# Latent attention on one core: queries, keys and values from the ranks as three products of rounded halves

## The reference, cut to what matters

```python
MLA_HEADS, MLA_Q_RANK, MLA_KV_RANK = 16, 384, 256
MLA_NOPE, MLA_ROPE, MLA_V = 64, 32, 64
def project(h, rotate):
    cq, ckv, kr, gate = split_last(h @ w_in, (MLA_Q_RANK, MLA_KV_RANK, MLA_ROPE, MLA_WIDTH))
    q = (rms_norm(cq, q_norm_g) @ w_uq).reshape(b, n, MLA_HEADS, MLA_NOPE + MLA_ROPE)
    kv = (rms_norm(ckv, kv_norm_g) @ w_ukv).reshape(b, n, MLA_HEADS, MLA_NOPE + MLA_V)
    ...
oc = attention_blocks(qc, kc, vc)                                   # context attends to itself
ox = attention_blocks(qx, concat([kc, kx]), concat([vc, vx]))       # input attends to both
return out(oc, gc), out(ox, gx)                                     # (o * silu(gate)) @ w_out
```

## Time and profile before

| | |
|---|---|
| time, median of 3 runs | 1775.43 us (1773.72 to 1776.09) |
| the profiled execution | 1776.33 us, of which the span is 1774.3 |
| TensorE (PE) busy | 1686.1 us, 95% of the span |
| VectorE (DVE) busy | 1323.5 us, 75% |
| ScalarE (ACT) busy | 777.0 us, 44% |
| DMA | 331.92 MB, mean 187 GB/s |

### The profile page before, as it was taken

The page is one execution under the profiler, slowest core; times in us unless marked ns, Lnnn a source line. Parts: engine busy times, 40 slices in busy tenths (PEclk is TensorE's granted clock), DMA queues, the critical chain, the costliest instruction groups (busy, mean ns, idle before and its releaser), DMA issues. The chain is left out here.

```text
span 1774.3 us, 30736 instructions
## 1 busy us (share of the span) xinstructions
PE 1686.1 (95%) x13112; PEld 1512.1 (85%) x13112; DVE 1323.5 (75%) x1965; ACT 777.0 (44%) x997; POOL 6.3 (0%) x14
## 2 busy tenths in 40 slices
PE   2999989999999999999899999999999999999998
PEld 2999978888899989999798779999886555759898
DVE  7777788855877778998878557999767768567844
ACT  2433365323633354343753327343652345355354
POOL 0000000000000000000000000000000000000000
PEclk9999999999999999999999999999999999999999
DMA  9868536351577746885364435776153200223102
GB/s 390 340 270 305 207 108 246 133 202 63 203 305 285 282 180 271 321 316 198 119 227 155 179 128 207 273 279 229 48 213 143 95 34 15 107 95 143 48 24 96
DMA packets 48807, 331.92 MB, mean 187 GB/s; under 512 B 5256, under 2 KB 8480, under 8 KB 9376
## 3 DMA queue, kind: packets, MB, share of 16 engines
q1 hardware_dynamic: 47808, 326.79, 48.2%
q0 software_dynamic: 864, 3.17, 0.7%
HBM read 328.87 MB, written 1.07 MB: 186 GB/s over the span
## 5 line engine op out<-in xcount | busy, mean ns | idle before, releaser
L347 PE MATMUL ps<-xhi,low 128*128 128x256 f32 x2048 | 499.5, 283 | 4.2 <-ACT xhi L1459 4.2
L347 PEld LDWEIGHTS ps<-xhi,low 128*128 128x128 f32 x2048 | 360.5, 190 | 6.4 <-ACT xhi L1459 5.6
L347 PE MATMUL ps<-xhi,whi_wk 128*128 128x256 f32 x1072 | 298.5, 288 | 40.5 <-ACT xhi L1459 38.7
L347 PE MATMUL ps<-xlo,whi_wk 128*128 128x256 f32 x1072 | 291.5, 281 | 0.0
L1459 ACT ACTIVATE wk<-ps 128x256 f32<-128x256 f32 (+5 forms) x219 | 108.1, 503 | 386.8 <-PE ps L347 320.8
L1459 ACT ACTIVATE whi_wk<-ring 128x2048 fp32r<-128x2048 f32 x100 | 191.6, 1918 | 195.3 <-DMA ring<-in_stream_dram 145.2
L347 PEld LDWEIGHTS ps<-xhi,whi_wk 128*128 128x128 f32 x1072 | 203.5, 195 | 43.2 <-issue 41.8
L2068 DVE TENSOR_TENSOR low<-ring,whi_wk 128x2048 fp32r<-128x2048 f32 (+1 forms) x101 | 228.4, 2264 | 6.6 <-ACT whi_wk L1459 6.6
L347 PE MATMUL ps<-wk 64*64 64x64 f32 (+10 forms) x2712 | 210.3, 262 | 5.8 <-ACT wk L1459 4.3
L347 PEld LDWEIGHTS ps<-wk 64*64 64x64 f32 (+4 forms) x2712 | 162.3, 146 | 55.0 <-issue 29.5
L347 PEld LDWEIGHTS ps<-xlo,whi_wk 128*128 128x128 f32 x1072 | 197.9, 189 | 0.0
(11 more groups left out here) (141 smaller groups left out, 2861.7 us busy)
## 6 DMA issues: line engine op xcount, KB each, us to landing
ring<-in_stream_dram SPq DMA_DIRECT2D x302, 1024.0 KB, 5.7
ring<-in_cond_dram SPq DMA_DIRECT2D x4, 1024.0 KB, 4.6
wk<-spread_dram POOLq DMA_DIRECT2D x4, 384.0 KB, 5.1
wk<-spread_dram POOLq DMA_DIRECT2D x2, 768.0 KB, 6.9
tab<-in_tab_dram SPq DMA_DIRECT2D x1, 1440.0 KB, 20.5
res<-in_xt_dram SPq DMA_DIRECT2D x1, 1024.0 KB, 17.5
res<-in_ct_dram SPq DMA_DIRECT2D x1, 1024.0 KB, 9.9
out_dram<-wk SPq DMA_DIRECT2D x4, 256.0 KB, 2.4
```

The lines of the kernel that those rows point to most:

```text
L347: last[0] = nc.tensor.matmul(o, l, r, start=start, stop=stop, skip_group_check=free)
```

## The change

Queries, keys and values are made as three float32r products too. For that the normed ranks get halves (`cqh`, five copies on ScalarE; `cql`, five subtractions on VectorE, in place of `cq`), and the chunks `uq` and `ukv` hold half as much: two heads instead of four, one group instead of two. Since half a chunk leaves half a place free, the high half goes to the upper 1024 floats of the chunk's own place and the low half over the raw weights (`up_high`, `up_low`). There are 8 `uq` chunks instead of 4 and 4 `ukv` chunks instead of 2, so SyncE issues 6 more loads of 1 MB. Two modulation chunks move back behind others in the ring. `cqh_later` is a copy of one of the high halves to another address, made on VectorE. Further, `x2lo` lies 512 floats lower.

```diff
-        LATE_AT = {2: (0,), 3: (1, 2), 4: (3, 4), 5: (5,), 6: (6, 7)}
+        LATE_AT = {2: (0,), 3: (1, 2), 4: (3,), 5: (4,), 6: (5, 6, 7)}
+        UP_SIZE = {"uq": 768, "ukv": 1024}
+        def half_places(n, size):
+            return low[:, n % RING, D:D + size], low[:, n % RING, 0:size]
...
                 def keys_values(g, i):
                     if i < 2:
                         for k in range(2):
-                            mm(b, w[:, k, at:at + P], cq[:, 3 + k, :], k == 0, k == 1)
+                            mm(b, hi[:, k, at], cq_hi(3 + k), k == 0, False)
+                            mm(b, lo[:, k, at], cq_hi(3 + k), False, False)
+                            mm(b, hi[:, k, at], cq_lo[:, 3 + k, :], False, k == 1)
...
-                    if g % 2 and i == 3:
+                    if i == 3:
                         held[0] = state["ukv_no"]
                         release()
...
+                def up_halves(kind, i, n):
+                    take(kind, i)
+                    eng.wait_ge(vector_done, step("ulow", kind, i))
+                    return [tiles(p, n) for p in half_places(held[0], UP_SIZE[kind])]
...
                 def queries(h):
-                    if h % 4 == 0:
-                        state["uq"] = take("uq", h // 4)[:, 0:1536].rearrange("p (k n) -> p k n", k=3)
+                    if h % 2 == 0:
+                        state["uq"] = up_halves("uq", h // 2, 256)
...
-                    if i == 5:
-                        next_keys(0)
...
                             if n == 10:
                                 eng.wait_ge(scalar_done, step("cqe", 1))
-                                eng.wait_ge(vector_done, step("cqn", m))
+                                eng.wait_ge(vector_done, step("cql", 4))
+                                next_keys(0)
...
-                        if h == 4:
-                            next_keys(1)
+                        if h % 4 == 0:
+                            next_keys(h // 4 + 1)
...  (ScalarE)
+                for t in (3, 4, 0, 1, 2):
+                    eng.wait_ge(vector_done, step("cqn", t))
+                    act(cq_hi(t), cq[:, t], ACT.Copy, "cqh", t).then_inc(scalar_done, 1)
                 for n in range(6, 14):
                     gate_out(n)
                     if n in (7, 9):
                         mla_high(5 + (n - 7) // 2)
+                        up_high(("ukv", "uq")[(n - 7) // 2], 0)
                     if n >= 10:
                         kv_copy(0, n - 10)
+                up_high("uq", 1)
+                up_high("ukv", 1)
...
+                    if h % 2 and h < 12:
+                        up_high("uq", h // 2 + 2)
+                    if h in (2, 6):
+                        up_high("ukv", h // 4 + 2)
...  (VectorE)
+                for t in (3, 4, 0, 1, 2):
+                    eng.wait_ge(scalar_done, step("cqh", t))
+                    tt(cq_lo[:, t], cq[:, t], cq_hi(t).bitcast(F32), SUB, "cql", t).then_inc(vector_done, 1)
...
                 mla_low(5)
                 mod_part(*LATE_MODS[3])
+                up_low("ukv", 0)
                 mla_low(6)
+                up_low("uq", 0)
...
                     mod_part(*LATE_MODS[c])
+                up_low("uq", 1)
                 q_part(1)
+                copy(cqh_later[:, :], cqh_first[:, :].bitcast(F32), "cqh_later").then_inc(vector_done, 1)
+                up_low("ukv", 1)
                 modulation(7)
...
+                    if h % 2 and h < 12:
+                        up_low("uq", h // 2 + 2)
+                    if h in (2, 6):
+                        up_low("ukv", h // 4 + 2)
```

More of the change, by code:

```diff
@@ L908, in keys_values, with next_keys @@
                         done.named("kv", g, i)
-                def next_keys(j):
-                    state["ukv"] = tiles(take("ukv", j), D)
+                def up_halves(kind, i, n):
+                    take(kind, i)
+                    eng.wait_ge(vector_done, step("ulow", kind, i))
+                    return [tiles(p, n) for p in half_places(held[0], UP_SIZE[kind])]
+                def next_keys(g):
+                    state["ukv"] = up_halves("ukv", g, 512)
                     state["ukv_no"] = held[0]
@@ L921, in queries @@
                 def queries(h):
-                    if h % 4 == 0:
-                        state["uq"] = take("uq", h // 4)[:, 0:1536].rearrange("p (k n) -> p k n", k=3)
+                    if h % 2 == 0:
+                        state["uq"] = up_halves("uq", h // 2, 256)
                         state["uq_no"] = held[0]
-                    w, hh = state["uq"], h % 4
+                    (hi, lo), hh = state["uq"], h % 2
+                    if h == 0:
+                        eng.wait_ge(vector_done, step("cql", 2))
+                    if h == 2:
+                        eng.wait_ge(vector_done, step("cqh_later"))
                     if h == 0:
@@ L1874, in mla, with up_high @@
                     act(tiles(sq2, 512)[:, t], res[:, t, :], ACT.Square, "sq7", t).then_inc(scalar_done, 1)
+            def up_high(kind, i):
+                n, size = found["chunk_no", kind, i][1], UP_SIZE[kind]
+                eng.wait_ge(landed[n % RING], loads(n))
+                act(half_places(n, size)[0], ring[:, n % RING, 0:size], ACT.Copy, "uround", kind, i).then_inc(scalar_done, 1)
             def high(*tag):
@@ L2565, in mla, with up_low @@
                 eng.wait_ge(scalar_done, step("cqr", m))
-                for t in range(5):
+                for t in (3, 4, 0, 1, 2):
                     g = col("q_norm", t) if t < 3 else col("kv_norm", t - 3)
-                    stt(cq[:, t], cq[:, t], g, rs2[:, 0:512] if t < 3 else rs2[:, 512:1024], MUL, MUL, *(("cqn", m) if t == 4 else ())).then_inc(vector_done, 1)
+                    stt(cq[:, t], cq[:, t], g, rs2[:, 0:512] if t < 3 else rs2[:, 512:1024], MUL, MUL, "cqn", t).then_inc(vector_done, 1)
+                eng.wait_ge(vector_done, done.count)
+                for t in (3, 4, 0, 1, 2):
+                    eng.wait_ge(scalar_done, step("cqh", t))
+                    tt(cq_lo[:, t], cq[:, t], cq_hi(t).bitcast(F32), SUB, "cql", t).then_inc(vector_done, 1)
+                def up_low(kind, i):
+                    n, size = found["chunk_no", kind, i][1], UP_SIZE[kind]
+                    hi, lo = half_places(n, size)
+                    eng.wait_ge(scalar_done, step("uround", kind, i))
+                    tt(lo, ring[:, n % RING, 0:size], hi.bitcast(F32), SUB, "ulow", kind, i).then_inc(vector_done, 1)
                 mla_low(5)
                 mod_part(*LATE_MODS[3])
+                up_low("ukv", 0)
                 mla_low(6)
+                up_low("uq", 0)
                 for c in range(4, 6):
@@ L2975, in chunk_of @@
         s = []
-        for h in range(4 * tag[1], 4 * tag[1] + 4):
+        for h in range(2 * tag[1], 2 * tag[1] + 2):
             s += [(96 * h, 96)] + [(96 * h + 64 + p, 8) for p in [8, 0, 24, 16]]
```

30 lines of the change are left out of this document (22 added, 8 removed).

## The result

The changed kernel takes 1781.4 us (median of 7 runs, 1779.38 to 1781.79), the kernel before beside it 1774.34 (7 runs, 1773.03 to 1776.48). The ratio is 1.0036, with a 95% interval of 1.0027 to 1.0046: **slower**, by 5 to 8 us. The forecast was 1780.4 us, slower, with a range of 1774.0 to 1784.5. It started from a kernel before of 1775.43 us and added 5.0; the medians here lie 7.1 apart. The profiled execution took 1781.52 us, its span 1779.4.

The account below looks back on a forecast made before the run. VectorE was taken to bound the odd head-loop passes, TensorE counting only in even ones. Terms +0.5 + 5.6 - 0.2 - 0.6 - 0.3 = +5.0 us on 1776.33 gave 1781.3, less 0.9 for the median: 1780.4, range 1774.0 to 1784.5.

Parts of the forecast that it names:

- `maxima(0)`: Start of the head loop: waits for `up_low` of ukv 1, starting at 1369.1 instead of 1368.59, +0.5 us.
- six `up_low` of 768 columns: Ends of passes 1, 3, 5, 7, 9, 11, ahead of the next maxima: 0.93 us each, uncovered, +5.6 us.
- passes 2 and 6: The `up_low` of 1024 columns replaces VectorE's wait for scores: -0.1 us each, -0.2 in all.
- passes 4 and 8: These passes wait for the keys, which take 0.32 us less each: -0.6 us.
- pass 10: This head-loop pass waits for scores and gets shorter: -0.3 us.
- the clock in passes 0 and 1: The forecast sum had no clock cost in these first passes; a clock case had chance 0.06.
- behind the loop: Behind pass 11 nothing changes; TensorE fills its waits there with terms of the output product.
- The rival of TensorE as the bound throughout: Whole kernel: all 12.5 us of TensorE savings come through, 1762.9 us; chance 0.06.
- Ahead of the loop: TensorE gains 2.18 us with queries 1; two new waits cost nothing, the third makes `maxima(0)` +0.5 us.
- TensorE's busy time: Whole profile: float32r products make TensorE's busy time about 12 us less.
- The halves hidden in VectorE's idle time: Head loop: subtractions hide while VectorE waits, so the loop only gains 1.5 us; 1774.4 us, chance 0.12.
- the late half: Ahead of the loop: late ScalarE copy and ukv 1 load start `maxima(0)` 2.7 us later; 1783.1 us, chance 0.16.

Follow-up runs that it names:

- the filled kernel: Changed kernel with twelve float32r matmuls of 512 columns, read by nobody, behind `keys_values(1, 0)` in pass 0; 1780.33 us, ratio 1.0030 to the kernel before.
- the kernel with both edits: Changed kernel with `up_low` of ukv 1 behind `maxima(0)` and the loop's `up_low` in VectorE's wait for the exponentials; 1774.27 us, ratio 0.9991 to the kernel before.
- the repeat of the changed kernel: The changed kernel timed once more, unedited, beside a kernel before of 1775.86 us; 1782.09 us, ratio 1.0036.
- the short queries: Kernel before with the third of three matmuls of each `queries(h)` left out, 13.7 us of TensorE work; 1776.8 us, ratio 1.0004.

## Why the prediction was right, point by point

| term | forecast | measured |
|---|---|---|
| `maxima(0)` | +0.5 | +0.62 (+0.64 with the start of keys) |
| six `up_low` of 768 columns | +5.6 | +5.04 |
| passes 2 and 6 | -0.2 | -0.35 |
| passes 4 and 8 | -0.6 | -0.66 |
| pass 10 | -0.3 | -0.31 |
| the clock in passes 0 and 1 | 0 | +1.70 |
| behind the loop | 0 | -0.92 |
| sum | +5.0 | +5.1 |

**VectorE bounds the odd passes, TensorE's work there counts nothing.** Right, and shown from both sides: six subtractions in the kernel before cost 5.3 us in the profile, and two matmuls for three in its queries gave 0 in passes 0 to 12. The margin is small: with 0.72 us less on VectorE in passes 3 and 7, passes 4 and 8 grew by 0.51 through TensorE. The rival of TensorE as the bound throughout fell.

**The size of an `up_low`.** 0.93 was taken, with 0.88 as the lower bound; measured 0.98 (first pass, with the clock's part taken off by the filled kernel), 0.73, 0.86, 0.74, 0.86 and 0.87. The subtraction is 0.98 start to start, above what I took, but `heads_low` ahead of it became 0.11 cheaper, 0.61 instead of 0.72, now that a subtraction stands behind it and not a reduction. Passes 3 and 7 are 0.13 shorter still: VectorE's wait for the exponentials is 1.87 there, and was 2.00.

**Ahead of the loop.** Right to 0.1 us: ScalarE's copy of ukv 1 at 1366.40 (forecast 1366.42), `maxima(0)` at 1369.23 (1369.1); `mla_high(5)` at 1326.01 (1326.2); keys (0, 0) at 1337.01 without a wait, although spared by only 0.4. The one wait that I had not seen is TensorE's 0.62 us for `cqh_later` ahead of the queries of head 2, which cost nothing, since the wait of 3.25 us stands behind it.

**TensorE's busy time** was to fall by about 12 us and fell by 8.2. Most of the difference is the clock: what runs at half clock counts as busy longer, scores 1 by 2.6 us and the 12 transposes behind them by 0.6, and without these 3.2 it would be 11.4.

**The halves hidden in VectorE's idle time** was a rival with "the written order puts it behind". That was so, and the other order gave it: the kernel with both edits took 1774.3, where the rival had 1774.4. That the two numbers agree is chance: the rival kept the late `maxima(0)` at +0.5, which the edits turned into -1.49, and it knew nothing of the 1.48 lost in pass 14.

**The clock was the failed step.** I wrote that "the gaps stay far shorter than the 4.3 us without work". I had worked out the gaps of the steady loop, 1.7 and 0.8 us, and not that of the first pass. There the 2.18 us that TensorE gains ahead of the loop and the 0.80 of the queries and keys of pass 0 all end up in one wait, since both stand ahead of scores 1 and those wait for VectorE. The rows had it: 0.38 us of wait before, 2.98 gained, 0.64 of later maxima, less 0.62 waited for `cqh_later` and 0.1, gives 3.25. Behind it the granted clock was 0.50. The price was 1.70, a third of what the rival had. The Trainium skill (TensorE: Matmul & The Clock Gate, Part 1) has an idle engine fall back to 1.2 GHz; the trace agrees here, where TensorE stood idle for 3.25 us and then ran at 0.50.

That the total still came within a us is partly luck: the clock's +1.70 stands against the 0.6 too much on the subtractions and the -0.92 at the end. The -0.92 did not come again: in the repeat of the changed kernel the end is 0.27 longer than in the kernel before, and the sum is +6.35. The medians say the same, +7.1 and in the repeat +6.2 where +5.0 was forecast; 1781.4 lies so near to 1780.4 also because the kernel before came out 1.1 faster than in the runs that the forecast started from.

**The upper end of the range.** The bounds that the prediction names add 0.3 (`up_low`) and 0.7 (`maxima(0)`) to 1780.4, which is 1781.4 and not 1783.5; no bound is given for passes 2 and 6 that would make the other 2.1. The stated end of 1784.5 then rests on the late half's 1783.1, a case that did not come.

## What to carry to other kernels

A saving on one engine is worth what it takes off the path, and it does not vanish elsewhere: it turns into a wait, and in a wait TensorE's clock may fall, so that 13.7 us less work came out at nothing. Look for where preparatory work stands: the same six subtractions cost 5 us at the end of a pass, and nothing some 6 us earlier in the same pass, inside a wait for another engine that the timeline shows in every pass. Where the wait on TensorE can't be removed, products of no use in it can be cheaper than the clock's fall: seven of them in pass 13 brought 1.4 us in the profile's pass 14 and 2.9 in the time, while the twelve in pass 0 moved the fall to pass 6 and brought nothing that the time shows for certain.

## What the hardware showed that was not expected

**Which wait lowers the clock can't be told from its length.** Behind waits of 3.25 (pass 0), 2.06 (pass 6), 1.89 us (pass 13) and, with the short queries, 2.25 us (pass 13) the clock fell; a wait of 1.90 us at 1507.51 in the changed kernel, its wait of 2.06 us at the start of pass 6, and one of 3.14 us at the start of the last block in one profile left it at 1.00. The price is 0.95 to 1.7 us each time in the loop, 3.1 in passes 13 and 14 of the kernel with the short queries, and 1.3 in the last block. An edit far ahead can move a fall from one place to another, as the filled gap did, from passes 0 and 1 to pass 6. I have no rule for it from these runs.

**Open.** The row of 264 float32r matmuls of 256 columns in the last block takes 31.49 us in the kernel before and in the repeat of the changed kernel, but 30.33 in the changed kernel's own profile, at a clock of 1.00 in both. Timeline, before and after, from its start to that of the next row:

```profile
1593.75 31.66 PE L347 MATMUL ps<-gtok,low 128*128 128x256 f32 x264
1625.24 5.13 PE L347 MATMUL ps<-ring,xa 128*128 128x256 f32 x23
```

```profile
1600.03 30.15 PE L363 MATMUL ps<-gtok,low 128*128 128x256 f32 x261
...
1630.36 7.07 PE L363 MATMUL ps<-ring,xa 128*128 128x256 f32 x32
```

It is the same code with the same operands. Nor is it known why the stages ahead of keys (0, 0) end up to 3 us apart from one profile to the next.
